# Input, parameter vectors and mixing weights handed over turned, and the first weight unit cast in two halves

## The reference, cut to what matters

```python
proj = x @ w_in                                  # 256x2048 @ 2048x10304, first product of the program
xbc = silu(causal_depthwise_conv(xbc, conv_w, conv_b))
dt = softplus(dt + dt_bias);  a = -exp(a_log)
y = y + d_skip * xs                              # then gate, norm * norm_g, @ w_out
...
ws = w_s * causal[None]                          # 16 groups of 128x128
mixed = einsum('gts,bnsgc->bntgc', ws, vc) + b_s
y = u * mixed * silu(zg)
```

## Time and profile before

| what | value |
|---|---|
| median of 3 runs | 2430.32 us |
| profiled execution | 2429.53 us |
| its span | 2428.3 us |
| PE busy | 2417.4 us, 19626 matmuls |
| DVE, ACT, POOL busy | 1572.8, 1243.5, 88.4 us |
| bytes moved | 467.93 MB, mean 193 GB/s |

### The profile page before, as it was taken

One profiled execution on the slowest core, in us unless ns is written; L12 is line 12 of the kernel. 1 busy time (PEld: TensorE's weight loads), 2 busy tenths in 40 slices (PEclk: granted clock), 3 DMA queues, 4 the chain that ended last, 5 costly groups with the idle time before them and its releaser, 6 DMA issues.

```text
span 2428.3 us, 45481 instructions
## 1 busy us (share of the span) xinstructions
PE 2417.4 (100%) x19626; PEld 2340.7 (96%) x19626; DVE 1572.8 (65%) x2109; ACT 1243.5 (51%) x1426; POOL 88.4 (4%) x68
## 2 busy tenths in 40 slices
PE   9999999999999999999999999999999999999998
PEld 9999999999999999999988899999999999999998
DVE  6778888866577766665575556656654555555556
ACT  5446665554454565554464445445444446455463
POOL 0001000100031000000000000000000000000002
PEclk9999999999999999999999999999999999999999
DMA  8666656557755655547767666666655576555645
GB/s 248 195 197 183 215 182 186 182 189 244 227 173 164 192 165 152 158 151 244 222 195 237 196 198 192 189 185 193 184 189 187 190 234 208 183 174 174 190 158 182
DMA packets 267434, 467.93 MB, mean 193 GB/s; under 512 B 18955, under 2 KB 70497, under 8 KB 265313
## 3 DMA queue, kind: packets, MB, share of 16 engines
q1 hardware_dynamic: 267233, 465.02, 62.0%
HBM read 452.18 MB, written 4.26 MB: 188 GB/s over the span
## 4 chain that ended last, share of the span: by engine, by line
PE 97%; DVE 1%; ACT 0%; DMA 0%; issue 0%; SPq 0%; ACTq 0%
PE G L703 91%; PE M L703 5%; PE M L716 1%; DMA RAW<-in_ssd_w_in 0%; DMA WS<-in_a_w_s 0%; DVE W1m L1547 0%; DVE W L1547 0%; DVE TT L2268 0%; DVE W2m L1547 0%; DVE W0m L1547 0%; DVE E L1640 0%; ACT W L1126 0%; ACT W0m L1126 0%; DVE RES L2263 0%; DVE E L1681 0%
## 5 line engine op out<-in xcount | busy, mean ns | idle before, releaser
L703 PE MATMUL G<-AA,W 128*128 128x256 f32 x7908 | 939.0, 277 | 1.1 <-DVE W L1547 1.0
L703 PEld LDWEIGHTS G<-AA,W 128*128 128x128 f32 x7908 | 915.7, 188 | 5.7 <-issue 2.7
L1547 DVE TENSOR_TENSOR W<-RAW,W 128x1024 fp32r<-128x1024 f32 x446 | 556.8, 1251 | 365.6 <-ACT W L1126 364.4
L1126 ACT CAST W<-RAW 128x1024 fp32r<-128x1024 f32 x446 | 464.9, 1047 | 463.2 <-PE G L703 454.0
L703 PE MATMUL G<-AA,WY 128*128 128x256 f32 x2508 | 304.3, 277 | 0.0
L703 PEld LDWEIGHTS G<-AA,WY 128*128 128x128 f32 x2508 | 293.0, 188 | 1.7 <-issue 1.4
L1547 DVE TENSOR_TENSOR WY<-RAW,WY 128x1024 fp32r<-128x1024 f32 (+1 forms) x112 | 142.2, 1272 | 74.1 <-ACT WY L1126 74.1
L703 PE MATMUL G<-W0m,YY 128*128 128x256 f32 x1512 | 183.7, 276 | 0.4 <-DVE W0m L1547 0.2
L703 PE MATMUL G<-W1m,YY 128*128 128x256 f32 x1512 | 183.1, 276 | 0.3 <-DVE W1m L1547 0.2
L703 PE MATMUL G<-W,YY 128*128 128x512 f32 x792 | 181.3, 389 | 0.0
L703 PE MATMUL G<-W2m,YY 128*128 128x256 f32 x1488 | 180.4, 276 | 0.0
(11 more groups left out here) (306 smaller groups left out, 2397.3 us busy)
## 6 DMA issues: line engine op xcount, KB each, us to landing
RAW<-in_a_w_in SPq DMA_DIRECT2D x192, 512.0 KB, 3.9
RAW<-in_ssd_w_in SPq DMA_DIRECT2D x160, 512.0 KB, 4.4
RAW<-in_b_w_in SPq DMA_DIRECT2D x128, 512.0 KB, 4.1
RAW<-in_dsa_w_in SPq DMA_DIRECT2D x72, 512.0 KB, 3.7
RAW<-in_ssd_w_out SPq DMA_DIRECT2D x64, 512.0 KB, 4.6
RAW<-in_dsa_w_out SPq DMA_DIRECT2D x64, 512.0 KB, 4.2
RAW<-in_a_w_out SPq DMA_DIRECT2D x64, 512.0 KB, 3.8
RAW<-in_b_w_out SPq DMA_DIRECT2D x32, 512.0 KB, 3.8
```

Source lines behind the costliest of these rows:

```text
L703: return e.matmul(o, l, r, start=start, stop=stop, skip_group_check=True)
L1126: e.copy(wh[:, 0:n], RAW[:, v % NR, 0:n]).then_inc(*up(cast_done, "cast", v))
L1547: e.tensor_tensor(wl[:, 0:n], RAW[:, v % NR, 0:n], wh[:, 0:n].bitcast(F), ALU.subtract).then_inc(*up(rest_done, "rest", v))
```

## The change

The host lays out three new inputs: x_turned (128 partitions, 16 blocks of features, 256 tokens), vectors (128x440, each parameter vector as columns, with d_skip spread and dt_bias and a_log doubled) and w_s_turned (s, group, t). The kernel loads x_turned into XS and takes heads and rests of AA straight from there; one load of 220 KB fills VC; WS arrives turned. The first part of x is issued by ACT, beside the first weight unit on SP, which now is SP's first load. PE's start holds 14 plain matmuls of the identity, and nothing else before the first unit. The first unit's cast and rest are done in halves of 512 columns, and PE starts its first 12 matmuls on the first half. The buffers VS, DB, dcol, dtb and alog go.

```diff
@@ sync_program, turn_in
-            x = A["x"][0].rearrange("(t p) n -> p t n", p=P)
-            for i, (c, w) in enumerate(((0, 256), (256, 256), (512, 512), (1024, 512), (1536, 512))):
-                e.dma_start(XS[:, :, c:c + w], x[:, :, c:c + w]).then_inc(*landed(x_parts[i], "x", i))
-                if i < NR:
-                    fetch(i)
-            for a, b, k, src in rows_in:
-                e.dma_start(VS[b:b + k, a, :], src).then_inc(*landed(d["rows_landed"], "rows"))
...
+            fetch(0)
+            for i, (k, z) in enumerate(X_PARTS):
+                if i > 0:
+                    e.dma_start(XS[:, k:z, :], A["x_turned"][:, k:z, :]).then_inc(*landed(x_parts[i], "x", i))
+                    if i < NR:
+                        fetch(i)
+            e.dma_start(VC[:, :], A["vectors"]).then_inc(*landed(d["vectors_landed"], "vc"))
@@ mix_load
-            e.dma_start(WS[:, :, :], A["a_w_s_2"][0, 2 * j:2 * j + 2].rearrange("g t s -> t g s")).then_inc(
+            e.dma_start(WS[:, :, :], A["w_s_turned"][:, 2 * j:2 * j + 2, :]).then_inc(
@@ tensor_program, unit
-            if part != 1:
+            if u == 0:
+                e.wait_ge(*on("rest", 0, 0))
+            elif part != 1:
                 e.wait_ge(*on("rest", u))
...
+                if u == 0 and j == 1:
+                    e.wait_ge(*on("rest", 0))
@@ tensor_program, turn_in
-            for k in range(0, 16, 2):
-                if k < 4:
-                    for _ in range(8 + k):
-                        transpose(M[:, 3, 0:P], ident[:, :], ident[:, :])
...
+            for _ in range(14):
+                mm(M[:, 3, 0:P], ident[:, :], ident[:, :], True, True)
@@ tensor_program
-        def mix_w(j):
...
@@ scalar_program
+                if v == 0:
+                    e.copy(wh[:, 0:n // 2], RAW[:, 0, 0:n // 2]).then_inc(*up(cast_done, "cast", 0, 0))
+                    e.copy(wh[:, n // 2:n], RAW[:, 0, n // 2:n]).then_inc(*up(cast_done, "cast", 0))
+                    continue
...
+            k, z = X_PARTS[0]
+            e.dma_start(XS[:, k:z, :], A["x_turned"][:, k:z, :]).then_inc(*landed(x_parts[0], "x", 0))
             for k in range(0, 16, 2):
-                e.wait_ge(*on("xt_t", k))
-                head(AA[:, k:k + 2, 0, :], M[:, bank.get(("xt", k), 0), :].rearrange("p (a n) -> p a n", a=2),
-                     "xt_h", k)
+                e.wait_ge(*on("x", (0, 1, 2, 2, 3, 3, 4, 4)[k // 2]))
+                head(AA[:, k:k + 2, 0, :], XS[:, k:k + 2, :], "xt_h", k)
@@ vector_program
+                if v == 0:
+                    for q in range(2):
+                        c = slice(q * (n // 2), (q + 1) * (n // 2))
+                        e.wait_ge(*(on("cast", 0) if q else on("cast", 0, 0)))
+                        e.tensor_tensor(wl[:, c], RAW[:, 0, c], wh[:, c].bitcast(F), ALU.subtract).then_inc(
...
+                rest(AA[:, k:k + 2, 1, :], XS[:, k:k + 2, :], AA[:, k:k + 2, 0, :]).then_inc(
@@ vector_program, mix_w
-            e.wait_ge(*on("ws_t", j))
+            e.wait_ge(*on("ws", j))
...
+            e.tensor_tensor(WM[:, :, :], WS[:, :, :], brc(triu[:, 0:P], 2), ALU.mult).then_inc(
```

More of the change, by code:

```diff
@@ L29 @@
 OUT_COLS = ((0, 768), (768, 1024), (1792, 256))
+VECTORS = (("cw", 192), ("cb", 48), ("ng", 32), ("lg", 32), ("lb", 32), ("qg", 4), ("kg", 2), ("n2", 32),
+           ("vg", 32), ("dskip", 32), ("dtb", 1), ("alog", 1))
+VCOL = {n: sum(k for _, k in VECTORS[:i]) for i, (n, _) in enumerate(VECTORS)}
+VCOLS = sum(k for _, k in VECTORS)
+X_PARTS = ((0, 2), (2, 4), (4, 8), (8, 12), (12, 16))
 TOKENS = ("o1", "o2", "o3", "o4", "cq", "v5", "v7")
@@ L207, in program @@
     pool_made = signal("pool_done")
+    x_parts = [signal(f"x{i}_landed") for i in range(5)]
     raw_here = [signal(f"raw{i}_landed") for i in range(NR)]
@@ L255, in program @@
     triu = place("triu", [P, 384])
-    VC = place("VC", [P, 4, P])
-    dcol = place("dcol", [P, 32])
+    VC = place("VC", [P, VCOLS])
     eps6 = place("eps6", [P, 2])
@@ L356, in used, with vc @@
         return UW if n > 1 and units[u][0][0] == "v" else units[u][3][0][1] * w
[L359 to L386, removed]
+    def vc(name, i=0, n=1):
+        c = VCOL[name] + i
+        return VC[:, c:c + n]
     def g_of(b):
@@ L1156, in dt_task @@
             nea = SZ[0:64, 1, 0:1]
-            e.wait_ge(*on("small"))
-            e.wait_ge(*on("vc_t"))
-            e.activation(nea, alog[:, :], ACT.Exp).then_inc(*up(act_made, "nea"))
+            e.wait_ge(*on("vc"))
+            e.activation(nea, vc("alog")[0:64], ACT.Exp).then_inc(*up(act_made, "nea"))
             yield
@@ L1559, in turn_in @@
                 e.wait_ge(*on("xt_h", k))
-                rest(AA[:, k:k + 2, 1, :], M[:, bank.get(("xt", k), 0), :].rearrange("p (a n) -> p a n", a=2),
-                     AA[:, k:k + 2, 0, :]).then_inc(*up(dve_made, "xt", k))
-                here(dve_made, "read", "xt", k)
+                rest(AA[:, k:k + 2, 1, :], XS[:, k:k + 2, :], AA[:, k:k + 2, 0, :]).then_inc(
+                    *up(dve_made, "xt", k))
                 if k % 4 == 2 or k == 0:
                     yield
-            e.wait_ge(*on("vc_t"))
-            for i, n in enumerate(nv):
-                e.tensor_copy(VC[:, i, 0:n], M[:, bank.get(("vc",), 0), i * P:i * P + n]).then_inc(
-                    *up(dve_made, "vc"))
-            here(dve_made, "read", "vc")
-            e.wait_ge(*on("small"))
-            for q in range(2):
-                e.tensor_copy(dcol[64 * q:64 * q + 64, :], DB[64 * q:64 * q + 64, q::2]).then_inc(
-                    *up(dve_made, "dcol"))
             yield
@@ L2417 @@
     nc = _bacc.Bacc("TRN2", target_bir_lowering=False, num_devices=1)
+    given = {name: inputs[name] for name in _INS}
+    given.update(_laid_out(inputs))
     arrays, args = {}, {}
-    for name in _INS:
-        a = _np.ascontiguousarray(inputs[name])
+    for name, value in given.items():
+        a = _np.ascontiguousarray(value)
         arrays[f"in_{name}"] = a
```

74 lines of the change are left out of this document (31 added, 43 removed).

## The result

| what | before | after |
|---|---|---|
| median of 10 runs each, same chip | 2430.78 us (2428.60 to 2432.53) | 2423.82 us (2423.51 to 2424.40) |
| profiled execution, its span | 2429.53, 2428.3 us | 2423.51, 2422.2 us |
| matmul records | 19626 | 19584 |

The ratio of the medians is 0.9971, 95% interval 0.9961 to 0.9981: 7.0 us faster.

What follows compares the result with a forecast made beforehand. The prediction took TensorE as the bound, busy 2417.4 of 2428.3 us. Its terms, 3.5 us at the start and 2.0 in the mixing stage, sum to 5.5, giving 2424.8 us from the median 2430.32; range 2422.4 to 2427.6.

Steps and rivals of the forecast that it cites:

- The first term: Start: the fifth weight unit begins on TensorE at 19.7 us instead of 23.20, gaining 3.5 us (ends 2.7 and 5.2).
- The count of bytes for the fifth unit's load: Start: 4.95 MB moved by 16.3 us, plus 1.2 lag, less 0.7 for larger packets, so landing at 16.8.
- The 2.9 us from there to TensorE: Start: time from the fifth unit's landing through its cast to the first rest of x behind it.
- The 0.7 us taken off for larger packets: Start: x in 2 or 4 KB pieces instead of 1 KB makes the fifth unit land 0.7 us earlier.
- The first unit: Start: load lands at 5.9 us, halved cast and rest take 1.2, so TensorE begins at 7.1 instead of 8.75.
- 14 matmuls at 0.21 us each end near 4.8: Start: the identity matmuls begin at 1.58 us and end near 4.8, leaving TensorE idle until 7.1.
- the clock rival: Start: idle until 7.1 us lowers the clock, first unit at half pace; first term 2.2, time 2426.1 us; chance 0.20.
- The rule weighed against the trace: Start: transposes don't raise the clock, so plain matmuls bring up to 2.7 us more, sum 8.2; the forecast counted nothing.
- The mixing term: Mixing stage: eight transpose pairs at 0.22 us leave TensorE, plus a late load's wait; 2.0 us (ends 1.2 and 2.4).
- The sum: Whole kernel: 3.5 at the start plus 2.0 in the mixing stage, 5.5 us; 2424.8 us against the median.
- Edits counted at nothing: Start: ACT's own load issue (0.44 us) and DVE's six small copies for VC and dcol, both taken as no gain or cost.

Runs made afterwards that it cites:

- e5: Changed kernel with the 16 transposes of w_s back on TensorE in the mixing stage, w_s loaded as before; span 2423.8 us against 2422.2.
- e2: Changed kernel with 7 identity matmuls at the start instead of 14; span 2423.0 us against 2422.2.
- f2: Changed kernel with casts and rests of x's later parts moved ahead of the third, fifth and seventh unit's cast; span 2422.3 us against 2422.2.
- f3: As f2, with the fifth unit's load also issued ahead of x's last part and the vectors; 2422.69 us, 0.9965 of the kernel before.
- e4: Changed kernel with x_turned laid out in 1 KB pieces instead of 2 or 4 KB, same bytes; span 2423.1 us against 2422.2.
- e8: Kernel before with only x turned by the host and 14 identity matmuls, 15 small vector loads kept, first unit whole; span 2432.1 us against 2428.3.
- f1: As e8, with 12 more identity matmuls behind the vectors' transposes, filling TensorE's idle stretch; span 2428.3 us against e8's 2432.1.
- e1: Changed kernel without any identity matmuls at the start; span 2423.2 us against 2422.2.
- e7: Kernel before with only the vectors' edit: one load for 15, their four transposes and six copies gone; span 2428.2 us against 2428.3.
- e6: As e5, but each pair of w_s transposes done twice (32 transposes); span 2426.6 us against the changed kernel's 2422.2.
- f0: The changed kernel run once more, beside f3 on the same chip; 2423.73 us, 0.9971 of the kernel before.

## Why the prediction was right, and where it was off

**The first term was right: 3.5 predicted, 3.4 at the mark.** The count of bytes for the fifth unit's load gave a landing at 16.8, its cast began at 16.77. To hit it that closely was luck, as the same list of loads gave casts from 16.29 (e5) to 17.11 (e2). But the count itself holds with the changed kernel's own bytes: 4.38 MB by 14.00, the other 0.57 at 400 GB/s until 15.4, and a lag of 1.4 where 1.2 was taken. The 2.9 us from there to TensorE measured 3.07 (19.84 less 16.77), so that the fifth unit came at 19.84 against 19.7. The load with its cast, its rest and one rest of x is what bound it, as the forecast said: with the casts of x out of that path (f2) the mark gains 0.6, with the load moved forward as well (f3) 0.8, and a slower x (e4) takes 0.85 away. The 0.7 us taken off for larger packets agrees with the bytes that e4 lacks, but the 247 GB/s from which it was worked out can't be taken for the rate of small pieces (e4).

**The first unit was off by 0.4, for a wrong reason.** The landing was earlier than taken (5.55 against 5.9). From there to a half that is ready it took about 1.4 against 1.2, since half a cast is 0.62 and not half of 1.05, and the half was ready at about 6.9. But "14 matmuls at 0.21 us each end near 4.8" was wrong: each of these plain f32 matmuls is two records in the trace, 28 in 6.12 us, and TensorE was still at it when the half was ready. How long the 28 take varies, from 5.11 us in e8 to 6.31 in f1 for the same list, and in f2 (5.24) they were over in time. It cost nothing at the fifth unit, which waited for its load. The same step also decided the clock rival. Slow matmuls do follow an idle start (e2 is just that case, e1 a worse one) and an idle stretch (e8), but the rival's condition, an idle TensorE from 4.8 to 7.1, did not come about. So the clock kept its pace for a reason that the forecast did not have, which was luck. The rival's price was too high where the case does come: nothing that shows in e2 and 0.9 in e1 at the mark against 1.3, since the fifth unit's load hides part of it.

**The rule weighed against the trace** would have made the sum 8.2; the gain at the marks is 5.9. The early transposes of the kernel before released the full pace for its first unit, as the plain matmuls do now, and the plain ones are not sure to be quicker at it: 28 records took 6.12 us, 0.22 each, where the transposes came 0.21 apart until 6.4 us. What speaks against the transposes is e7 alone, where much the same ones left the first unit slow. That rule (the Trainium skill, TensorE: Matmul & The Clock Gate, Part 4: PE-mode transpose) finds no support in either of the two kernels.

**The mixing term was mis-sized: 2.0 predicted, 2.6 measured.** It was 8 times the transposes' own 0.22 plus 0.3. The runs put a visit at 0.28 instead of 0.22, since about 0.08 of it is a fixed price (e5 and e6). That makes 8 times 0.28 = 2.2, and the late load of the earlier trace rows cost 0.33 where 0.24 was taken (the 0.2 and "a little"). Its upper end, 2.4, was short too. DVE's new wait for the load put no stall on TensorE, as taken.

**The sum** was then 5.5 against 6.0 (3.4 and 2.6), or 6.1 of span. Against medians it reads 7.0 in one comparison and 6.2 in the other. What lies over 6.1 is mostly the kernel before's: its median lay 1.25 us over its profiled execution, the changed kernel's 0.31 over its own. Its runs spread over 4 us and those of the changed kernel over 0.9 in the first comparison, over 6.4 and 1.4 in the second. The varying wait near 500 us can make part of such a spread; that it makes all of it was not tried.

**Edits counted at nothing** were nothing at the marks: the copies for VC and dcol, and ACT's own load issue. The edit of the vectors was not nothing: without it x's edit loses 2.6 us (e8), because 15 small loads hold back the fifth unit's. The forecast had this in its words, by placing the load and not TensorE on the path, but gave no price to either edit alone.

## What to carry to other kernels

When two edits each lift one of two bounds that lie close together, neither shows its worth alone, and one may do harm: look at the mark where both bounds meet. Ask also what the same kernel gives when nothing is changed: at such a mark, executions differed here by up to 0.5 us through landings alone. Work taken off TensorE ahead of a late load turns into idle time, and the idle time can cost more than the work did; put the load forward, or fill the gap. A visit of a few foreign matmuls in a long stream costs its own time and about 0.08 us more here.

## What was not expected of the hardware

- A plain f32 matmul of 128x128 by 128 columns is two records: 14 in the program are 28 in the trace, 24 of them (12 in the program) took 2.94 us at full pace in f1. A transpose of the same block is one.
- After 2.58 us of idle time in e8 the granted clock read 0.50, the 1.2 GHz level, from 23 to 29 us. In the first microseconds of e1, e2 and e7 the matmuls ran at half of the later pace while the granted clock read 1.00: there, only the count of matmuls shows it.
- The same early loads land at different times in different kernels: the fifth unit's cast began at 16.29 in e5, 16.36 in e6, 16.62 in e1, 16.77 in the changed kernel and in f0, 16.86 in f2 and 17.11 in e2, though SyncE's list is the same up to there. Differences of up to 0.5 us in the start can be that.
- ScalarE's heads of x take 0.62 us a piece from XS, where the same shape took 0.59 from PSUM in e7.
